# Splitting x times g_mix before its norm is known, and multiplying the norm's root in later, in the opening of a two-block transformer kernel

## The chip, the cores and the metric

The kernel runs on one core of one Trainium2 chip, in one launch. The metric is device time in microseconds (us), the median of several runs. The engines are TensorE (PE, matmuls; PEld its weight loads), VectorE (DVE), ScalarE (ACT), GpSimd (POOL) and SyncE (SP, which only issues transfers here).

## The reference, cut to what matters

Two transformer blocks over 1024 tokens of width 1024, in fp32. The first one begins so:

```python
def rms_norm(x, g):
    xf = x.astype(jnp.float32)
    y = xf * lax.rsqrt(jnp.mean(xf * xf, axis=-1, keepdims=True) + EPS)
    return (y * g.astype(jnp.float32)).astype(x.dtype)
...
        u = rms_norm(h, g_mix[l]) @ w_in[l]
        # u is cut into qa, ka, va (differential attention: 4 units of 128 columns each)
        # and qs, ksb, vs (stick-breaking attention: 4 units of 128 columns each)
        qa = apply_partial_rope(qa, cos, sin)
        ka = apply_partial_rope(ka, cos, sin)
        ya = diff_attention(qa, ka, va, lam, g_subln[l], lam_init)
        yb = stick_breaking_attention(qs, ksb, vs)
```

The root of the norm is one number per token. It is the same for all columns of a projection, and the rotation (apply_partial_rope) is linear, so it may be multiplied in before the projection or behind it.

## The kernel before, in words

**Layout.** Activations lie feature-major: 128 partitions hold features, the free dimension holds the 1024 tokens, in 8 slices k of 128 features and two halves h of 512 tokens. x is `hT`. Every product is made of three fp32r matmuls per slice (`product`, lines 184 to 186): the operand is split into a rounded high part and a low part (the rest), and high by high, high by low and low by high are summed. A chunk is one projection of 128 columns for 512 tokens, so 8 slices of three matmuls. It is named (what, unit, half): ("q",0,1) is q of unit 0, second half. "r" is a product with the rotation's matrix (parts 0 and 1 for q, 2 and 3 for k), "t" the transposition of v, "ada" and "o" are small ones. Chunks alternate between two PSUM banks; chunk n waits until chunk n-2 was taken out. Chunks run in the order of `CHUNK_ORDER`, which begins with `FIRST_CHUNKS`: q00, k00, q01, r00, r01, k01, r02, r03, v00, v01, t00, t01 (what, unit, part).

**Weights.** SP brings a panel of 512 KB into `w_raw`, GpSimd makes its high part (L233) and its low part (L194), into one of two places. A place is free again when the first matmul of the next panel has run (`weight_free`). SP asks for a panel when the one before was split.

**Opening.** The transfers of x come in 16 pieces. ScalarE squares each slice (L290) into `yT`; VectorE adds slices 4 to 7 of the first half (L328); TensorE sums over features with a matmul by ones (L337, L319 for the second half, put between the slices of q00); ScalarE takes Ln and Exp of the mean (`norm_root`, L345, L349). Only then VectorE multiplies x by g_mix and the root (L393), ScalarE takes the high part (L190), VectorE the low part (L194, in place of x), and TensorE starts the slice of q00. Then come k00, q01 and so on. VectorE also makes the angles (L2921 to L2936), ScalarE their sine and cosine (L3165, L3166), and VectorE rotates q and k of unit 0 (`rope_dve`, L703 to L706, three instructions of 1024 columns each for q and for k). The first scores of the attention (`da_scores(0)`, L744) wait for both.

**Attention stages.** 32 steps of differential attention (4 units of 8 steps, `da_pe`, `da_dve`, `da_act`) and then 48 of stick-breaking (4 units of 12 steps, `sb_...`) work on unit i while TensorE fills its time with the chunks of unit i+1. In every step TensorE issues scores, the chunks, a transposition of weights (L756, L911) and the product with v (L767, L929), in an order written out by hand; so do the other engines. In these stages all chunks are taken from PSUM by ScalarE (`chunk_act`, L678 for q and k, L674 for v, L670 for t), at the end of its step. VectorE's step: maxima, a third of a panel of the adaptive projection (`ada_dve`, four instructions from L691 to L697), rotation in steps 5 and 6, weights (L822, L824, L829); in stick-breaking two scans (L1013), a subtraction (L1019), `ada_dve` in some steps.

Of the kernel before, what the change touches and what calls it, by code (L numbers as in the profile page):

```python
# [99 lines left out]
def program(nc, xT_d, memT_d, pos_d, vec_d, const_d, bias_d, lora_d, w_d, out_d):  # L100
# [7 lines left out]
    with ctx:  # L108
# [166 lines left out]
        MIX_SUM = 3  # L275
        NORM_ADDS = {n: [(k, 0) for k in range(MIX_SUM + 1, KC)] if n == "mix" else [(k, h) for k, h in NORM_SQUARES[n] if k % KC and not summed_late(n, k, h)] for n in NORM_SQUARES}
        NORM_ROOTS = {"mix": [0, 1], "mem": [0], "x": [0, 1], "mlp": [0, 1], "fin": [0, 1], "fin1": [0, 1], "post": [0, 1]}
        NORM_OUT = {n: [(k, h) for h in (NORM_ROOTS[n]) for k in range(KC)] for n in NORM_SQUARES}
# [36 lines left out]
        def norm_pe_chunk(pe, n, h, k):  # L315

            c = norm_cols(n, h)
            pe.wait_ge(S("norm_sq_ready"), norm_at(NORM_SQUARES, n, (k, h)))
            m = pe.matmul(PS[:, NB + c.start:NB + c.stop], cst("ones"), norm_sq[n](k)[:, c], start=(k == 0), stop=(k == KC - 1))  # L319
            if k == KC - 1:  # L320
                m.then_inc(S("norm_summed"), 1)

        def mix_add(dve, k):
            dve.wait_ge(S("norm_sq_ready"), norm_at(NORM_SQUARES, "mix", (k, 0)))
            if k > MIX_SUM + 1:
                dve.wait_ge(S("norm_added"), norm_at(NORM_ADDS, "mix", (k - 1, 0)))
            c, sq = norm_cols("mix", 0), norm_sq["mix"]
            dve.tensor_tensor(sq(MIX_SUM)[:, c], sq(MIX_SUM)[:, c], sq(k)[:, c], ALU.add).then_inc(S("norm_added"), 1)  # L328

        def mix_sum_pe(pe):  # L330
            c = norm_cols("mix", 0)
            for k in range(MIX_SUM + 1):
                if k < MIX_SUM:
                    pe.wait_ge(S("norm_sq_ready"), norm_at(NORM_SQUARES, "mix", (k, 0)))
                else:
                    pe.wait_ge(S("norm_added"), norm_at(NORM_ADDS, "mix", (KC - 1, 0)))
                m = pe.matmul(PS[:, NB + c.start:NB + c.stop], cst("ones"), norm_sq["mix"](k)[:, c], start=(k == 0), stop=(k == MIX_SUM))  # L337
            m.then_inc(S("norm_summed"), 1)
# [154 lines left out]
        n_rs = arena[:, at_da:at_da + T]  # L493
# [107 lines left out]

        def chunk_done(c):

            return S("proj_evac"), CHUNK[c] + 1
# [16 lines left out]
        def chunk_pe(pe, c, part=None):  # L621
            n, (what, w, h) = CHUNK[c], c
            b = bank(n % 2)
            if n >= 2 and part != 1:
                pe.wait_ge(S("proj_evac"), n - 1)
# [19 lines left out]
            else:  # L645
# [4 lines left out]
                if w == 0 and what == "q":  # L650
                    def ready(k):
                        if h == 0:
                            norm_pe_chunk(pe, "mix", 1, k)
                        wait_split(pe, "mix", h)(k)
# [4 lines left out]
        def chunk_act(act, c):  # L659
            n, (what, w, h) = CHUNK[c], c  # L660
            if what == "w" or c == ("ada", UNITS - 1, 0):
                return
# [10 lines left out]
            elif what == "v":  # L673
                e = act.activation(raw[:, 4 + h, :], b, ACT.Copy)  # L674
            else:
                x = UNIT_PANEL[what]
                dst = (raw_qk if w < N_DA else heads(w))[x]
                e = act.activation(dst[:, cols], b, ACT.Copy, scale=0.125 if what == "q" else 1.0)  # L678
# [157 lines left out]
        def da_dve(dve, g):  # L836
# [11 lines left out]
            da_weights(dve, g)  # L848

# [6 lines left out]
        AT = [t.rearrange("p (h k) -> p h k", h=2) for t in (ar.take(T), pos_f)]  # L856
# [57 lines left out]
        def sb_values(pe, g):  # L914
# [12 lines left out]
            for b in range(n):  # L927
                for hd in range(2):
                    m = pe.matmul(PS[64 * hd:64 * hd + 64, 7 * HALF + t % 4 * P:7 * HALF + (t % 4 + 1) * P],  # L929
                                  values_of(w)[1][:, lo + b, 64 * hd:64 * hd + 64], AT[g % 2][:, hd, b * P:(b + 1) * P],  # L930
# [2575 lines left out]
```

## Time and profile before

| | us |
|---|---|
| median of 3 runs | 2319.09 (2318.38 to 2323.09) |
| the profiled execution: its time | 2321.39 |
| the profiled execution: its span | 2319.6 |
| TensorE busy | 2229.3 (96%) |
| VectorE busy | 1363.4 (59%) |
| ScalarE busy | 951.7 (41%) |
| GpSimd busy | 700.3 (30%) |
| first scores (L744) start at | 73.59 |

Times in the rows are microseconds from the start of the span. The opening is what lies ahead of the first scores. Differential attention runs up to about 330 us, stick-breaking up to about 620 us; the rest of the span is not touched by the change. "Busy" of TensorE includes matmuls at half clock and small ones, so 96% does not say that nothing can be gained.

### The profile page before, as it was taken

What the parts mean: (1) busy time and instruction counts of PE and PEld (TensorE: products, weight loads), DVE (VectorE), ACT (ScalarE), POOL (GpSimd) and SP (SyncE); (2) the same over time, 40 slices, a digit from 0 to 9 for tenths busy, and PEclk for the clock granted to TensorE, in tenths of its full rate; (3) what the DMA queues carried; (4) which work ended last, traced back from release to release, by engine and by line L of the source; (5) the groups of instructions that cost most, each with busy time, mean ns of one, the idle gap of its engine ahead of it and who ended that gap; (6) DMA issues with size and microseconds to landing.
All of it is one profiled execution on the core that took longest, in us unless ns stands there. A gap on an engine that the chain in (4) does not pass through costs nothing.

```text
span 2319.6 us, 36425 instructions
## 1 busy us (share of the span) xinstructions
PE 2229.3 (96%) x14780; PEld 1761.7 (76%) x14780; DVE 1363.4 (59%) x1775; ACT 951.7 (41%) x1688; POOL 700.3 (30%) x436
## 2 busy tenths in 40 slices
PE   7999999998999999999999999999899999999997
PEld 4777766666689887778888888888676787778885
DVE  6767647667677444575664575423508476567554
ACT  4443457677535223253344234233416412264321
POOL 2312211211221223345564564322141133222231
PEclk9999999999999999999999999999999999999999
DMA  3211101113023101111111111112120011100022
GB/s 132 73 55 55 37 28 55 55 46 119 26 93 119 37 28 37 46 37 55 64 36 54 54 54 45 55 46 96 64 79 28 19 37 37 39 19 13 4 110 82
DMA packets 38555, 125.80 MB, mean 54 GB/s; under 512 B 3856, under 2 KB 4368, under 8 KB 37776
## 3 DMA queue, kind: packets, MB, share of 16 engines
q1 hardware_dynamic: 33936, 103.30, 13.2%
q10 hardware_dynamic: 4480, 20.49, 2.3%
q8 instruction: 106, 1.74, 0.3%
q14 instruction: 33, 0.27, 0.0%
HBM read 114.34 MB, written 8.91 MB: 53 GB/s over the span
## 4 chain that ended last, share of the span: by engine, by line
PE 85%; DVE 8%; ACT 5%; issue 2%; DMA 0%; ACTq 0%; DVEq 0%
PE PS L184 22%; PE PS L186 22%; PE PS L185 22%; PE PS L2261 2%; PE PS L744 2%; PE PS L767 1%; PE PS L1200 1%; PE PS L929 1%; PE PS L894 1%; DVE arena L1013 1%; PE PS L911 1%; PE PS L312 1%; PE PS L1871 1%; DVE arena L393 1%; PE PS L1731 1%
## 5 line engine op out<-in xcount | busy, mean ns | idle before, releaser
L184 PE MATMUL PS<-u_r,w_hi 128*128 128x512 f32 x1184 | 480.5, 406 | 16.1 <-DVE h L581 3.6
L233 POOL TENSOR_TENSOR w_hi<-w_raw,const 128x1024 fp32r<-128x1024 f32 x77 | 152.0, 1974 | 1120.8 <-PE PS L184 1016.5
L186 PE MATMUL PS<-u_r,w_lo 128*128 128x512 f32 x1184 | 464.3, 392 | 0.0
L194 POOL TENSOR_TENSOR w_lo<-w_raw,w_hi 128x1024 fp32r<-128x1024 f32 (+1 forms) x143 | 331.3, 2317 | 325.4 <-ACT w_hi L190 310.5
L185 PE MATMUL PS<-arena_r,w_hi 128*128 128x512 f32 (+1 forms) x888 | 332.7, 375 | 0.0
L184 PEld LDWEIGHTS PS<-u_r,w_hi 128*128 128x128 f32 x1184 | 224.0, 189 | 72.8 <-DVE arena_r L194 6.5
L186 PEld LDWEIGHTS PS<-u_r,w_lo 128*128 128x128 f32 x1184 | 223.8, 189 | 48.1
L184 PE MATMUL PS<-h_r,w_hi 128*128 128x512 f32 x512 | 208.1, 406 | 4.7 <-DVE u_r L401 4.4
L185 PE MATMUL PS<-y_r,w_hi 128*128 128x512 f32 x512 | 201.3, 393 | 0.0
L186 PE MATMUL PS<-h_r,w_lo 128*128 128x512 f32 x512 | 199.6, 390 | 0.0
L1526 DVE TENSOR_TENSOR h<-h,PS 128x512 f32<-128x512 f32 x288 | 181.7, 682 | 21.8 <-PE PS L186 17.6
L185 PEld LDWEIGHTS PS<-arena_r,w_hi 128*128 128x128 f32 x888 | 167.8, 189 | 29.7 <-issue 0.7
L185 PE MATMUL PS<-h_r,w_hi 128*128 128x512 f32 x384 | 150.0, 391 | 0.0
L185 PE MATMUL PS<-u_r,w_hi 128*128 128x512 f32 x384 | 150.0, 391 | 0.0
L1013 DVE TENSOR_TENSOR_SCAN arena<-arena 128x512 f32<-128x512 f32 (+3 forms) x96 | 105.7, 1142 | 70.8 <-ACT arena L987 70.8
L1512 DVE TENSOR_TENSOR arena<-arena 128x512 f32<-128x512 f32 x60 | 51.4, 880 | 154.3 <-ACT arena L1445 154.3
L184 PE MATMUL PS<-y_r,w_hi 128*128 128x512 f32 x344 | 134.3, 390 | 0.0
L186 PE MATMUL PS<-y_r,w_lo 128*128 128x512 f32 x344 | 133.9, 389 | 0.0
L184 PEld LDWEIGHTS PS<-h_r,w_hi 128*128 128x128 f32 x512 | 96.1, 188 | 37.3 <-DVE u_r L401 8.1
L190 ACT ACTIVATE w_hi<-w_raw 128x1024 fp32r<-128x1024 f32 (+1 forms) x73 | 64.3, 881 | 132.4 <-PE PS L184 85.7
L185 PEld LDWEIGHTS PS<-y_r,w_hi 128*128 128x128 f32 x512 | 97.2, 190 | 20.4 <-issue 1.0
L186 PEld LDWEIGHTS PS<-h_r,w_lo 128*128 128x128 f32 x512 | 96.2, 188 | 20.7
(434 smaller groups left out, 4283.2 us busy)
## 6 DMA issues: line engine op xcount, KB each, us to landing
w_raw<-in_w SPq DMA_DIRECT2D x174, 512.0 KB, 3.4
arena<-in_w SPq DMA_DIRECT2D x10, 512.0 KB, 5.1
h<-in_xT ACTq DMA_DIRECT2D x1, 4096.0 KB, 14.6
u<-parked_stream ACTq DMA_DIRECT2D x1, 4096.0 KB, 12.9
out<-arena SPq DMA_DIRECT2D x16, 256.0 KB, 2.0
parked_stream<-h ACTq DMA_DIRECT2D x6, 512.0 KB, 2.6
h<-in_xT SPq DMA_DIRECT2D x8, 256.0 KB, 7.1
h<-in_xT ACTq DMA_DIRECT2D x8, 256.0 KB, 8.9
```

What stands on the lines that cost most here:

```text
L184: first = pe.matmul(out, a[0], b[0], start=start, stop=False)
L185: pe.matmul(out, a[0], b[1], start=False, stop=False)
L186: return first, pe.matmul(out, a[1], b[0], start=False, stop=stop)
L190: return e.activation(out, x, ACT.Copy)
L194: return e.tensor_tensor(out, x, hi_part.bitcast(F), ALU.subtract)
L233: pool.tensor_tensor(out, src, cst("ones")[:, 0:1].broadcast_to([P, D]), ALU.mult).then_inc(S("w_high"), 1)
L312: m = pe.matmul(PS[:, at + c.start:at + c.stop], cst("ones"), norm_sq[table](k)[:, c], start=(x == 0), stop=(x == len(parts) - 1))
L744: pe.matmul(bank(2 + 2 * c, 2)[:, lo:hi], q[r, s * P:(s + 1) * P], k[r, lo:hi], start=True, stop=(hi < kw))
L1013: m = dve.tensor_tensor_scan(sums, sums, ab[:, g % 2, hd, :cols][:, ::-1], 0.0 if whole else sp[:, (g - 1) % 2, hd, 0:1], ALU.add, ALU.add)
L1512: dve.tensor_tensor(*(st_block(f, x) for f in (out, a, b)), op).then_inc(S("hid_ready"), 1)
L1526: dve.tensor_tensor(dst, dst, bank((7 * j + p) % 8), ALU.add if sign > 0 else ALU.subtract).then_inc(S("dn_evac"), 1)
L2261: m = pe.matmul(out[half(cp), h, t, :], a(h, t)[half(cp), :], b(h, t)[half(cp), :], start=start, stop=stop)
```

## The change

1. **The split comes ahead of the root.** ScalarE makes the high part of x times g_mix directly from x (an activation with g_mix as its scale), and squares the slice right behind it. VectorE makes the low part in one instruction, x times g_mix minus the high part. The multiplication by the root (L393, 16 instructions) goes.
2. **The root is multiplied in later.** The sine and cosine tables are multiplied by it (two instructions of 1024 columns), which covers q and k of units 0 to 3. Every v, and q and k of units 4 to 7, are taken from PSUM by VectorE with a multiplication by the root (`scaled_chunk_dve`), where ScalarE copied them before: 16 v chunks and 16 of q and k. In `da_dve` this stands behind the weights of the step, in `sb_dve` behind the subtraction and `ada_dve`. For unit 0 the order on VectorE is: tables, rotation of q, v00, rotation of k, v01.
3. **Sums.** First half: TensorE sums slices 0 to 3 ahead of q00 and the rest (three additions on VectorE) ahead of q01. Second half: six additions on VectorE, two sums on TensorE ahead of k01, in place of eight sums between the slices of q00. The roots are taken by ScalarE behind the chunks q01 and r01.
4. **Order on ScalarE.** The second half's slices 0 to 3, then the chunk q00, then slices 4 to 7.
5. **Panel 1** (k of unit 0) is brought at the start, ahead of the late pieces of x, to a place of its own (`early_raw`), and split by GpSimd without a wait for TensorE; before, its split began with q00's first matmul.
6. The root lies in the place of the positions (`pos_f`) up to the end of stick-breaking, so its second weight buffer (`AT`) moves elsewhere.

```diff
         def split_unit_panel(pool, m):
-            if m > 0:
+            if m == 1:
+                pool.wait_ge(S("mem_in"), 16)
+                pool.sem_inc(w_in[0], 16)
+                pool.tensor_tensor(w_hi[:, 1, :], early_raw, cst("ones")[:, 0:1].broadcast_to([P, D]), ALU.mult).then_inc(S("w_high"), 1)
+                pool.wait_ge(S("w_high"), 2)
+                low(pool, w_lo[:, 1, :], early_raw, w_hi[:, 1, :]).then_inc(S("w_split"), 1)
+                return
+            if m > 1:
                 pool.wait_ge(S("weight_free"), m + CREDIT)
...
+        MIX_SUMS = {0: [(4, 5), (4, 6), (4, 7)], 1: [(0, 1), (2, 3), (4, 5), (6, 7), (0, 2), (4, 6)]}
...
+        def scaled(c):
+
+            return c[0] == "v" or (c[0] in "qk" and c[1] >= N_DA)
+
         def chunk_done(c):
 
-            return S("proj_evac"), CHUNK[c] + 1
+            same = [x for x in CHUNK_ORDER if scaled(x) == scaled(c)]
+            return S("proj_scaled" if scaled(c) else "proj_evac"), same.index(c) + 1
+
+        def scaled_chunk_dve(dve, c):
+
+            n, (what, w, h) = CHUNK[c], c
+            cols = slice(h * HALF, (h + 1) * HALF)
+            dve.wait_ge(S("proj_mm"), n + 1)
+            if what == "v":
+                e = dve.tensor_tensor(raw[:, 4 + h, :], bank(n % 2), n_rs[:, cols], ALU.mult)
+            elif what == "q":
+                e = dve.scalar_tensor_tensor(heads(w)[0][:, cols], bank(n % 2), 0.125, n_rs[:, cols], ALU.mult, ALU.mult)
+            else:
+                e = dve.tensor_tensor(heads(w)[1][:, cols], bank(n % 2), n_rs[:, cols], ALU.mult)
+            e.then_inc(S("proj_scaled"), 1)
...
             if n >= 2 and part != 1:
-                pe.wait_ge(S("proj_evac"), n - 1)
+                pe.wait_ge(*chunk_done(CHUNK_ORDER[n - 2]))
...
             da_weights(dve, g)
+            for c in da_chunks(i, s):
+                if scaled(c):
+                    scaled_chunk_dve(dve, c)
...
             load_main(0)
+            sync.dma_start(early_raw, w_d[2, :, :]).then_inc(S("mem_in"), 16)
             for k in range(4):
                 sync.dma_start(hT[:, k, HALF:T], xT_d[:, k, HALF:T]).then_inc(S("x_late"), 16)
-            load_main(1)
...
-            split_dve(dve, "mix", 0, in_(hT), in_u, in_h, mix)
+            for h in range(2):
+                for k in range(KC):
+                    mix_low(k, h)
+                for to, k in MIX_SUMS[h]:
+                    mix_add(dve, h, to, k)
...
-            dve.wait_ge(S("ang_ready"), 3)
+            dve.wait_ge(*norm_ready("mix", 1))
+            for x, table in enumerate((sinT, cosT)):
+                dve.wait_ge(S("ang_ready"), x + 2)
+                dve.tensor_tensor(table, table, n_rs, ALU.mult).then_inc(S("ang_step"), 1)
+            dve.wait_ge(S("ang_step"), 9)
             for x in range(2):
                 rope_dve(dve, 0, x)
-            dve.wait_ge(S("cact_ready"), 1)
+                scaled_chunk_dve(dve, ("v", 0, x))
+            dve.wait_ge(S("cact_ready"), 2)
...
+            def mix_part(k, h):
+                lo, hi = split_cols("mix", h)
+                act.activation(in_u(k, lo, hi), hT[:, k, lo:hi], ACT.Identity, scale=vcol("g_mix", k)).then_inc(S("split_high"), 1)
+                norm_square(act, "mix", k, h, hT[:, k, lo:hi])
...
             for k in range(KC):
-                mix_square(k, 1)
-                mix_split(0, [k])
-            norm_root(act, "mix", 1, n_rs)
-            for c in FIRST_CHUNKS:
+                mix_part(k, 1)
+                if k == 3:
+                    chunk_act(act, ("q", 0, 0))
+            act.wait_ge(S("const_in"), 16)
+            for c in FIRST_CHUNKS[1:]:
                 chunk_act(act, c)
-                if c == ("q", 0, 0):
-                    mix_split(1, range(KC))
+                if c in (("q", 0, 1), ("r", 0, 1)):
+                    mix_root(0 if c[0] == "q" else 1)
...
-            mix_sum_pe(pe)
-            pe.wait_ge(S("lam_exp"), 1)
+            mix_sum_pe(pe, 0, range(4), True, False)
             for c in FIRST_CHUNKS:
+                if c == ("q", 0, 1):
+                    mix_sum_pe(pe, 0, [4], False, True)
+                if c == ("k", 0, 1):
+                    mix_sum_pe(pe, 1, [0, 4], True, True)
```

## Rows read from the trace of the kernel before

**Rows 1.** The page: the chain that ended last, share by engine.
```profile
PE 85%; DVE 8%; ACT 5%; issue 2%; DMA 0%; ACTq 0%; DVEq 0%
```

**Rows 2.** Stretches: busy of each engine (x instructions), PEclk, DMA share, GB/s.
```profile
16.00:18.00 2.00, 0.37 (x1) 0.37 (x2) 1.38 (x2) 0.00 (x0) 0.00 (x0) 0.50 0.98 413
...
24.00:26.00 2.00, 2.00 (x6) 1.20 (x4) 2.00 (x3) 1.27 (x3) 1.62 (x1) 0.50 0.00 0
...
40.00:50.00 10.00, 9.41 (x40) 6.88 (x39) 9.87 (x17) 5.55 (x9) 0.00 (x0) 1.00 0.01 2
```

**Rows 3.** Timeline of the opening: start, duration, engine, line, [idle before <-releaser].
```profile
8.17 2.19 ACT L290 ACTIVATE y<-h 128x512 f32<-128x512 f32 x4
8.85 4.59 PE L337 MATMUL PS<-y,const 128*128 128x512 f32 x6 [3.23 <-ACT y L290]
...
12.29 2.35 POOL L194 TENSOR_TENSOR w_lo<-w_raw,w_hi 128x1024 fp32r<-128x1024 f32 x1
12.30 5.27 DVE L328 TENSOR_TENSOR y<-y 128x512 f32<-128x512 f32 x4 [7.58 <-ACT y L290]
...
38.36 0.40 PE L184 MATMUL PS<-u_r,w_hi 128*128 128x512 f32 x1
```

**Rows 4.** Instructions on the tile h: min/median/max ns, first and last start.
```profile
L393 DVE SCALAR_TENSOR_TENSOR h<-h,vec,arena x16: 736/742/2383, 21.3 to 47.6; 128x512 f32<-128x512 f32 x16
```

**Rows 5.** Timeline from k01's first matmul to the first scores.
```profile
52.33 0.56 PE L184 MATMUL PS<-u_r,w_hi 128*128 128x512 f32 x1
...
55.98 2.39 POOL L194 TENSOR_TENSOR w_lo<-w_raw,w_hi 128x1024 fp32r<-128x1024 f32 x1
...
62.16 1.89 POOL L233 TENSOR_TENSOR w_hi<-w_raw,const 128x1024 fp32r<-128x1024 f32 x1 [3.80 <-DMA w_raw<-in_w]
...
62.93 1.14 ACT L3166 ACTIVATE arena<-arena,const 128x1024 f32<-128x1024 f32 x1
...
64.16 3.46 DVE L703 TENSOR_TENSOR arena<-arena 128x1024 f32<-128x1024 f32 x1 [8.05 <-ACT arena L3166]
...
69.92 1.22 DVE L703 TENSOR_TENSOR arena<-arena 128x1024 f32<-128x1024 f32 x1
...
73.59 0.49 PE L744 MATMUL PS<-arena 64*128 64x128 f32 x4 [1.25 <-DVE arena L706]
```

**Rows 6.** Line 1526, a VectorE instruction with one operand in PSUM: min/median/max ns.
```profile
L1526 DVE TENSOR_TENSOR h<-h,PS x240: 678/680/690, 1033.5 to 1393.1; 128x512 f32<-128x512 f32 x120
```

**Rows 7.** Timeline of steps 5 and 6 of unit 0, differential attention.
```profile
111.78 3.25 POOL L194 TENSOR_TENSOR w_lo<-w_raw,w_hi 128x1024 fp32r<-128x1024 f32 x1
112.82 3.30 DVE L706 TENSOR_TENSOR y<-y,arena 128x1024 f32<-128x1024 f32 x1
...
116.94 1.02 DVE L829 SCALAR_TENSOR_TENSOR arena<-arena,er 128x768 f32<-128x768 f32 x1
...
118.65 0.60 PE L756 MATMUL PS<-const,arena 128*128 128x128 f32 x4
```

**Rows 8.** Timeline of the border between two units of stick-breaking.
```profile
401.52 0.61 ACT L674 ACTIVATE arena<-PS 128x512 f32<-128x512 f32 x1
...
403.81 1.05 PE L715 MATMUL PS<-const,arena 128*128 128x128 f32 x8
...
404.17 1.22 DVE L1019 TENSOR_TENSOR arena<-PS,arena 128x1024 f32<-128x1024 f32 x1
...
406.08 0.50 PE L184 MATMUL PS<-u_r,w_hi 128*128 128x512 f32 x1 [1.23 <-ACT arena L670]
```

**Rows 9.** Timeline of the border ahead of the last unit of stick-breaking.
```profile
544.23 1.05 PE L715 MATMUL PS<-const,arena 128*128 128x128 f32 x8
...
546.24 1.22 DVE L1019 TENSOR_TENSOR arena<-PS,arena 128x1024 f32<-128x1024 f32 x1
...
547.52 0.70 PE L894 MATMUL PS<-arena 64*128 64x256 f32 x4 [0.62 <-DVE arena L1019]
...
567.92 0.50 PE L184 MATMUL PS<-u_r,w_hi 128*128 128x512 f32 x1 [2.93 <-DVE h L581]
```

More of the change, by code:

```diff
@@ L272, in summed_late @@
             return n in ("mlp", "fin", "post") and h == 1 and k % KC >= KC - 2
-        MIX_SUM = 3
-        NORM_ADDS = {n: [(k, 0) for k in range(MIX_SUM + 1, KC)] if n == "mix" else [(k, h) for k, h in NORM_SQUARES[n] if k % KC and not summed_late(n, k, h)] for n in NORM_SQUARES}
+        MIX_SUMS = {0: [(4, 5), (4, 6), (4, 7)], 1: [(0, 1), (2, 3), (4, 5), (6, 7), (0, 2), (4, 6)]}
+        NORM_ADDS = {n: [(k, h) for h in range(2) for _, k in MIX_SUMS[h]] if n == "mix" else [(k, h) for k, h in NORM_SQUARES[n] if k % KC and not summed_late(n, k, h)] for n in NORM_SQUARES}
         NORM_ROOTS = {"mix": [0, 1], "mem": [0], "x": [0, 1], "mlp": [0, 1], "fin": [0, 1], "fin1": [0, 1], "post": [0, 1]}
-        NORM_OUT = {n: [(k, h) for h in (NORM_ROOTS[n]) for k in range(KC)] for n in NORM_SQUARES}
+        NORM_OUT = {n: [(k, h) for h in (NORM_ROOTS[n]) for k in range(KC)] if n != "mix" else [] for n in NORM_SQUARES}
         norm_sq = {}
@@ L330, in mix_sum_pe, with mix_add @@
[L330 to L338, printed above, removed]
+        def mix_add(dve, h, to, k):
+            c, sq = norm_cols("mix", h), norm_sq["mix"]
+            dve.wait_ge(S("norm_sq_ready"), norm_at(NORM_SQUARES, "mix", (k, h)))
+            before = [x for x in MIX_SUMS[h][:MIX_SUMS[h].index((to, k))] if x[0] in (to, k)]
+            if before:
+                dve.wait_ge(S("norm_added"), norm_at(NORM_ADDS, "mix", (before[-1][1], h)))
+            dve.tensor_tensor(sq(to)[:, c], sq(to)[:, c], sq(k)[:, c], ALU.add).then_inc(S("norm_added"), 1)
@@ new lines, in mix_sum_pe @@
+        def mix_sum_pe(pe, h, parts, start, stop):
+            c = norm_cols("mix", h)
+            for k in parts:
+                if stop and k == parts[0]:
+                    pe.wait_ge(S("norm_added"), norm_at(NORM_ADDS, "mix", (MIX_SUMS[h][-1][1], h)))
+                elif not stop:
+                    pe.wait_ge(S("norm_sq_ready"), norm_at(NORM_SQUARES, "mix", (k, h)))
+                m = pe.matmul(PS[:, NB + c.start:NB + c.stop], cst("ones"), norm_sq["mix"](k)[:, c], start=start and k == parts[0], stop=stop and k == parts[-1])
+            if stop:
+                m.then_inc(S("norm_summed"), 1)
@@ L672, in chunk_act @@
                 e = act.activation(osq[:, cols], b, ACT.Ln, bias=cst("eps"), scale=1.0 / P)
-            elif what == "v":
-                e = act.activation(raw[:, 4 + h, :], b, ACT.Copy)
             else:
                 x = UNIT_PANEL[what]
-                dst = (raw_qk if w < N_DA else heads(w))[x]
-                e = act.activation(dst[:, cols], b, ACT.Copy, scale=0.125 if what == "q" else 1.0)
+                e = act.activation(raw_qk[x][:, cols], b, ACT.Copy, scale=0.125 if what == "q" else 1.0)
             e.then_inc(S("proj_evac"), 1)
@@ L855, in program, with sb_at @@
         Eb = ar.take(2 * T).rearrange("p (b h k) -> p b h k", b=2, h=2)
-        AT = [t.rearrange("p (h k) -> p h k", h=2) for t in (ar.take(T), pos_f)]
+        at_even = ar.take(T)
+        def sb_at(g):
+            t = at_even if g % 2 == 0 else yT[:, 7, :] if g < 3 * SB_N else arena[:, 14 * T + 3 * P:15 * T + 3 * P]
+            return t.rearrange("p (h k) -> p h k", h=2)
         def sb_item(g):
@@ L1030, in sb_dve @@
                     ada_dve(dve, *at[j, s])
-                if j == 3:
-                    for c in sb_chunks(j, s):
-                        if c[0] != "t":
-                            late_chunk_dve(dve, c)
+                for c in sb_chunks(j, s):
+                    if scaled(c):
+                        scaled_chunk_dve(dve, c)
+                    elif j == 3 and c[0] != "t":
+                        late_chunk_dve(dve, c)
             else:
```

57 lines of the change are left out of this document (22 added, 35 removed).

## Prediction

> **What bounds the kernel now.** I read the chain that ended last first. It runs over TensorE for 85% [rows 1], so the change pays only where TensorE starts earlier or waits less. Then I read the granted clock by stretches, the timeline of the opening engine by engine, and the waits of TensorE in the two attention stages.
>
> In the opening the reader sees a chain that is not TensorE's: x lands, ScalarE squares, VectorE adds, and here it stands still behind GpSimd. Its four additions take 5.27 us [rows 3], of which the first waits for the low part of panel 0, which began 0.01 us before it and took 2.35. Then come the sum, the root, and three passes per slice on two engines. k00's first matmul is at 38.36 [rows 3], k01's at 52.33, the first scores at 73.59 [rows 5]. From there TensorE hardly waits.
>
> The trace shows one thing that matters for everything below: a VectorE instruction with two operands in SBUF and a GpSimd instruction exclude each other, and they take turns. In rows 7 GpSimd's low part (3.25 in place of 2.35) waited for the VectorE instruction ahead, and VectorE's next (3.30 in place of 1.22) waited for GpSimd. The low part beside the cosine did the same to L703: 3.46 against 1.22 [rows 5]. With an operand in PSUM this is not so: 240 instructions of L1526 took 0.678 to 0.690 [rows 6].
>
> **Part 1, up to k01.** ScalarE now makes two passes per slice. Four squares took 2.19, so 0.53 each [rows 3], 1.07 per slice; slices 0 to 7 are squared by 9.3, 10.4, ... 16.8. TensorE's sums of slices 0 to 3 take 2 passes each of 0.77 to 0.86 (six passes took 4.59 [rows 3]), so from 9.4 to 16.2, which is before it can do much else.
>
> The low parts are one instruction each of 0.74 (the form of L393 [rows 4]), the first at 9.4. From 10.3 GpSimd splits panel 0, and now panel 1 directly behind it: 1.89 + 2.35 + 1.89 + 2.39 = 8.5 us [rows 3, 5] of GpSimd work. Both engines are never idle together and take turns, so the last of seven remaining low parts ends at 10.3 + 8.5 + 7 x 0.64 = 23.3. Without this collision it would be 17.5. q00's last slice ends at 24.4 (at half clock at 26). So k00 starts at 24.4 where it started at 38.36.
>
> From k00's to k01's first matmul it took 13.97 us: 48 matmuls at 0.235 (40 in 9.41 [rows 2]) are 11.3, four passes for the rotations 1.7, and about 1 us is waiting for low parts. Now the wait is gone (the low parts of the second half end at about 31, when q01 starts), and six passes of sums at 0.43 are added, 2.6 us. That is 15.6, and k01 starts at 40.0: 12.3 us earlier. Hidden under TensorE here: the additions on VectorE (9 x 0.7), ScalarE's roots (2 x 1.4), panel 1's split. Panel 1's transfer delays the late pieces of x by 0.5 MB, about 2.5 us by the rate of this stretch; ScalarE then needs them at 17 and has until 24. If that cover went, ScalarE would be late by that much at most.
>
> **Part 2, from k01 to the first scores.** Before, the cosine ended 11.7 us after k01's start (52.33 to 64.07 [rows 5]). The same queue stands ahead of it, so it ends at 51.7 and the sine at 50.6. Then comes a longer chain on VectorE: two tables (2 x 1.2), rotation of q (3 x 1.2), v00 (0.68 [rows 6]), rotation of k (3 x 1.2), v01 (0.68), 11.0 us together, where it was 7.0. And again GpSimd meets it: the low part of panel 2 ends at about 46.5, the raw panel 3 lands 3.8 us later (58.37 to 62.16 [rows 5]), so both halves of panel 3's split fall on the two table instructions. Two blocks, 4.0 us; bounds: 0 and 4.3. v01 is out at 65.5, TensorE turns t01 in 0.6, the first scores start at 66.1. Gain 7.5 (between 6 and 11.5).
>
> What is late next: TensorE. It has done v01's matmuls at 58.2 and then waits 2.5 us for v00 and 4 us for v01, for t00 and t01 need them. In the trace an idle stretch of such length, from 13.4 (the end of the six passes) to 17.6 (the end of the additions) [rows 3], goes with a granted clock of 0.50, at 1.2 GHz, from 16 until 26, four us after TensorE was busy again [rows 2]. I charge the same: four us at half clock on matmuls that bound the step, 2 us (bounds 0 and 2.5). The Trainium skill ("TensorE: Matmul & The Clock Gate", Part 1) calls the throttled state the default, which only activity releases; by that rule the new wait costs this second charge, without it the opening would be worth the whole first gain. The trace agrees with it at 16 to 26 us. Opening: -7.5 + 2 = -5.5 (between -11.5 and -2.5).
>
> VectorE's step 0 starts about 1 us later against the scores than before, as ScalarE loads two tables behind t01. TensorE's next need of it is more than 1 us away; nothing.
>
> **Part 3, the chunks taken by VectorE.** The instruction costs 0.68 instead of 0.60 and isn't blocked [rows 6]; what matters is its place in the queue. In differential attention it follows the weights. In step 5 these end at 117.96, so v0 is out at 118.6, and TensorE asks for that bank after L756 of 118.65, at 119.1 [rows 7]: no wait, by 0.5 us. The other steps have more room. Nothing.
>
> In stick-breaking it follows the subtraction of its step. At a border between units ScalarE took v1 at 401.52, and TensorE turned v at 403.81 [rows 8]. Now v1 waits for the subtraction, which ends at 405.4, and is out at 406.1; t0 follows, ScalarE takes it, and q's first matmul is at 407.3 instead of 406.08. 1.2 us, twice. At the third border VectorE is busy without a pause: v0's 0.68 shifts the subtraction of 546.24 to 546.9, v1 is out at 548.8, t1 ends at 549.4 instead of 545.3, and the scores of 547.52 come 1.7 us behind it, at 551.1 [rows 9]. ScalarE stands behind them. The stretch up to the wait of 2.93 at 567.92 is bound by ScalarE and VectorE, so 3.3 us go through to the end. In three steps VectorE's extra 0.68 is on a chain that ScalarE's saved 0.5 nearly pays back: 0.2 x 3 = 0.6. Sum +6.3, less 0.3 for what ScalarE saves elsewhere: +6.0 (between +2.5 and +8).
>
> **The sum.** -7.5 + 2 + 6.0 = +0.5 on the profiled execution's 2321.39, so 2321.9. That execution lies 2.3 above the median of the runs, 2319.09; against the median I say 2319.5. About 0.2%, 4.6 us, is what a measurement of this kernel can tell from no change.
>
> **The rivals.** *The opening keeps its gain (faster).* GpSimd's split of panel 3 misses the tables, for instance because panel 2 was split earlier: 4 us more. Then TensorE's waits are 1 to 3 us and the clock may hold, 2 us more; the sum is -5.5, 2313.6. For it: the blocks come from a coincidence of about 1 us. Against: GpSimd's start hangs on TensorE and SP in the same way as the sine does, so the meeting place is steady. 0.27.
>
> *v of differential attention comes too late (slower).* In step 5 the margin is 0.5 us. If VectorE is later by more, TensorE waits ahead of v1 in each of three units, and by one more turn with GpSimd (2 us and more, as in rows 7) this is 3 x 2 = 6 us: 2325.5. It decides from 0.5 us of lateness. Against: GpSimd has already blocked VectorE twice in this very step. 0.16.
>
> *The high parts don't wait for a root, but nothing comes earlier.* If TensorE stayed at half clock through q00 and k00, k01 would start 1.6 + 5.6 = 7.2 us later than I say (24 matmuls at twice 0.235), and the opening be worth nothing: +7.7, 2326.8. Against: the sums from 9.4 on keep TensorE busy. It shares the chance above; its milder form, q00 alone, is in my forecast's range (2321.1).
>
> Forecast (little change, between 2315 and 2323.5): 0.57. Faster by over 0.2% 0.27, within 0.2% 0.57, slower 0.16. The range for 8 in 10 takes most of the faster case and half of the slower: 2311 to 2324.
>
> **What would show it.** In the profile after: low parts of 0.74 with four or so of 2.5 to 3 us between 10 and 23 us; k00's first matmul near 24.4, k01's near 40; two table multiplications of 3 us near 51 to 57; L744 first near 66 with idle time of TensorE ahead of it and a granted clock of 0.5 behind; TensorE waiting ahead of the transposition of v at the borders of units, and the third border 3 us longer. If the first scores start under 63, or the borders show no wait, the number is too high; if TensorE waits ahead of the second half of v in differential attention, it is too low.

## The result, and the profile after

The changed kernel takes 2328.6 us (median of 9 runs, 2324.53 to 2332.52), the kernel before 2320.94 in the runs beside it (9 runs, 2318.38 to 2323.09). The ratio is 1.0034, with a 95% interval from 1.0026 to 1.0043: slower by 7.7 us. I had said 2319.5, and a range that ends at 2324. Of the 9.1 us between, 1.9 lie in the kernel before, whose median I took from 3 runs (2319.09) and which is 2320.94 with 9; the other 7.2 are the change's. The profiled execution of the changed kernel took 2328.1.

The shares on the profile's page have hardly moved, and show nothing of it [rows 1]:

```profile
PE 2228.9 (96%) x14770; PEld 1762.3 (76%) x14770; DVE 1385.0 (60%) x1798; ACT 936.3 (40%) x1656; POOL 703.0 (30%) x436
...
PE 85%; DVE 8%; ACT 5%; issue 2%; DMA 0%; SPq 0%; DVEq 0%; ACTq 0%
```

VectorE has 21.6 us more work and ScalarE 15.4 less, TensorE as much as before.

The opening does what was said, within about 1 us at each mark. These are rows of its timeline after the change (start, duration, engine, line, and in brackets the idle time before):

```profile
11.04 11.78 DVE L2943 SCALAR_TENSOR_TENSOR h_r<-h,vec,u_r 128x512 fp32r<-128x512 f32 x7 [0.38 <-ACT y L297]
...
12.51 2.68 POOL L194 TENSOR_TENSOR w_lo<-w_raw,w_hi 128x1024 fp32r<-128x1024 f32 x1
...
17.58 2.70 POOL L194 TENSOR_TENSOR w_lo<-arena,w_hi 128x1024 fp32r<-128x1024 f32 x1
...
24.53 0.49 PE L184 MATMUL PS<-u_r,w_hi 128*128 128x512 f32 x1
...
40.28 0.79 PE L184 MATMUL PS<-u_r,w_hi 128*128 128x512 f32 x1
...
50.30 1.89 POOL L233 TENSOR_TENSOR w_hi<-w_raw,const 128x1024 fp32r<-128x1024 f32 x1 [3.92 <-DMA w_raw<-in_w]
...
51.74 4.87 DVE L2977 TENSOR_TENSOR arena<-arena,pos_i 128x1024 f32<-128x1024 f32 x2 [5.15 <-ACT arena L3205]
...
60.17 0.68 DVE L621 TENSOR_TENSOR arena<-PS,pos_i 128x512 f32<-128x512 f32 x1
...
61.00 0.63 PE L731 MATMUL PS<-const,arena 128*128 128x128 f32 x4 [1.93 <-DVE arena L621]
...
65.13 1.09 PE L731 MATMUL PS<-const,arena 128*128 128x128 f32 x4 [3.49 <-DVE arena L621]
66.15 0.80 PE L760 MATMUL PS<-arena 64*128 64x128 f32 x4
```

The seven low parts share the time with GpSimd, q00 ends and k00 starts at 24.5 (38.36 before [rows 3]), k01 starts at 40.28 (52.33 [rows 5]), GpSimd meets the two tables, TensorE waits 1.93 and 3.49 for v, and the first scores start at 66.15 (73.59 [rows 5]). What is lost is lost in stick-breaking. Here are rows of its timeline. L731 turns v, L184 begins a chunk, L918 are scores, L1043 is VectorE's subtraction, L621 and L625 are its copies of v and k with the root multiplied in. They answer to [rows 8, 9]:

```profile
399.64 0.68 DVE L621 TENSOR_TENSOR arena<-PS,pos_i 128x512 f32<-128x512 f32 x1
...
400.38 1.97 PE L731 MATMUL PS<-const,arena 128*128 128x128 f32 x8 [2.08 <-DVE arena L621]
...
402.18 0.79 PE L184 MATMUL PS<-u_r,w_hi 128*128 128x512 f32 x1
...
472.77 1.10 PE L731 MATMUL PS<-const,arena 128*128 128x128 f32 x8 [2.08 <-DVE arena L621]
...
520.04 1.22 DVE L1043 TENSOR_TENSOR arena<-PS,arena 128x1024 f32<-128x1024 f32 x1
...
521.18 0.68 DVE L625 TENSOR_TENSOR arena<-PS,pos_i 128x512 f32<-128x512 f32 x1
...
521.91 0.50 PE L184 MATMUL PS<-u_r,w_hi 128*128 128x512 f32 x1 [2.41 <-DVE arena L625]
...
523.68 0.63 PE L184 MATMUL PS<-u_r,w_hi 128*128 128x512 f32 x1
524.10 0.63 PE L185 MATMUL PS<-h_r,w_hi 128*128 128x512 f32 x1
...
548.48 1.22 DVE L1043 TENSOR_TENSOR arena<-PS,arena 128x1024 f32<-128x1024 f32 x1
...
549.62 0.68 DVE L621 TENSOR_TENSOR arena<-PS,pos_i 128x512 f32<-128x512 f32 x1
...
550.45 1.09 PE L731 MATMUL PS<-const,arena 128*128 128x128 f32 x4 [3.82 <-DVE arena L621]
...
554.14 0.70 PE L918 MATMUL PS<-arena 64*128 64x256 f32 x4
```

Four times TensorE stands still for a copy of VectorE's, for 2.08, 2.08, 2.41 and 3.82 us. Stretches of the same execution (busy of PE, PEld, DVE, ACT, POOL, then the granted clock, DMA share and GB/s) show what follows such a wait:

```profile
22.00:24.00 2.00, 2.00 (x6) 1.61 (x5) 1.90 (x4) 0.76 (x2) 0.00 (x0) 0.50 0.52 197
...
66.00:68.00 2.00, 2.00 (x10) 1.47 (x9) 0.00 (x0) 1.73 (x2) 0.11 (x1) 0.50 0.00 0
68.00:70.00 2.00, 2.00 (x8) 1.60 (x7) 1.59 (x3) 1.96 (x5) 1.92 (x2) 0.72 0.00 0
...
398.00:404.00 6.00, 3.92 (x16) 3.11 (x15) 2.94 (x5) 2.67 (x6) 0.95 (x1) 0.72 0.01 3
472.00:478.00 6.00, 4.99 (x36) 3.89 (x36) 1.36 (x4) 1.35 (x3) 3.22 (x2) 1.00 0.00 0
518.00:524.00 6.00, 3.59 (x21) 2.92 (x20) 5.80 (x6) 3.59 (x7) 1.51 (x1) 0.92 0.00 0
524.00:530.00 6.00, 6.00 (x35) 3.85 (x35) 2.44 (x2) 1.39 (x2) 3.56 (x2) 0.79 0.01 3
...
548.00:554.00 6.00, 3.56 (x24) 2.90 (x24) 2.91 (x5) 1.77 (x4) 0.00 (x0) 0.72 0.91 391
```

After three of the four waits the granted clock falls; after the second it doesn't (1.00). In the kernel before it was 1.00 in the stretches of the first and of the last wait:

```profile
398.00:404.00 6.00, 5.86 (x46) 4.81 (x45) 3.77 (x4) 5.17 (x9) 0.00 (x0) 1.00 0.00 0
...
548.00:554.00 6.00, 4.39 (x41) 2.68 (x40) 4.09 (x6) 6.00 (x10) 0.00 (x0) 1.00 1.02 436
```

A way to read both kernels side by side is to take the start of each step's scores in the changed kernel and subtract that of the kernel before (73.59 at the first step, 547.52 at step 37 of stick-breaking, and so on; steps are counted through the four units, from 0). The difference stays the same over many steps and then jumps; a jump upwards is a loss with a place, one downwards a gain. Below, "first" and "next" are the first two steps of differential attention, "SB 0" and "SB 47" the first and last of stick-breaking, and the four columns between are the jumps from step 12 to 13, 24 to 25, 32 to 33 and 36 to 37 (the first, second and fourth stand at the borders between units). All from one execution each, in us:

| kernel | first | next | SB 0 | 12-13 | 24-25 | 32-33 | 36-37 | SB 47 | median |
|---|---|---|---|---|---|---|---|---|---|
| changed | -7.44 | -6.10 | -6.56 | +2.42 | +1.27 | +3.79 | +4.83 | +6.33 | 2328.6 |
| changed, again (e8) | -7.98 | -6.51 | -6.97 | +2.42 | +3.70 | +4.82 | +4.87 | +9.43 | 2329.77 |
| e1, copies alone | +0.19 | +0.21 | -0.21 | +2.33 | +3.66 | +4.80 | +5.15 | +16.13 | 2335.18 |
| e2, opening alone | -9.09 | -8.05 | -9.39 | -0.01 | -0.01 | +0.02 | -0.09 | -9.82 | 2312.99 |
| e3, copies first | -7.74 | -6.35 | -6.78 | -0.01 | -0.02 | -0.31 | +0.51 | -7.65 | 2311.89 |
| e4, panel 3 later | -11.18 | -6.32 | -5.75 | +2.50 | +2.26 | +3.85 | +5.09 | +9.85 | 2332.28 |
| e5, borders first | -8.71 | -7.40 | -7.87 | +0.02 | -0.02 | +3.80 | +1.05 | -2.33 | 2317.5 |
| e6, k first, once | -8.41 | -7.23 | -8.05 | +3.73 | +2.54 | -0.31 | +5.15 | +0.87 | 2325.77 |
| e7, e3 and v first | -7.85 | -5.75 | -6.50 | +0.00 | -0.01 | -0.30 | +0.50 | -6.93 | 2313.9 |

The jumps left out of the table that are over 0.8 us lie at fixed steps too. They don't hang on the place of the copies in stick-breaking, for e3 has them as well: from first to next, then -1.4, +1.6 and -1.6 at the borders between the units of differential attention, and +1.6 from step 2 to 3 of stick-breaking (e6 lacks this one and has -1.65 from step 0 to 1; some kernels lack others). The clock goes with them, in either kernel. At the -1.4 and the -1.6 it is the kernel before that runs slower, 0.73 from 132 to 138 us and 0.75 from 262 to 268, where the changed kernel has 1.00. At the +1.6 between them it is the changed kernel, 0.72 from 190 to 196, where the kernel before has 1.00. At the last one it is 0.76 from 339 to 345 us in the changed kernel and 0.74 in e8, and 1.00 in the kernel before. Twice one of 1.1 to 1.5 stands behind step 40 (+1.07 in e4, -1.54 in e2).

Behind stick-breaking the two kernels run the same program, and the difference still wanders, by 0.4 to 3.5 us: +6.33 becomes +6.7 at the end of the span for the changed kernel (2326.3 less 2319.6), -9.82 becomes -12.0 in e2 (2307.6 less 2319.6), -2.33 becomes +0.7 in e5 (2320.3). So medians say what a version is worth, and jumps say where.

### The profile page after: what moved, and what is told of

It is laid out like the page before. It is cut to its first block, busy times and chain, and to the rows that moved or that the text cites. A ratio compares the mean times of both kernels' runs of the same rounds, so it can differ in the third digit from the quotient of the medians.

```text
span 2326.3 us, 36417 instructions
## 1 busy us (share of the span) xinstructions
PE 2228.9 (96%) x14770; PEld 1762.3 (76%) x14770; DVE 1385.0 (60%) x1798; ACT 936.3 (40%) x1656; POOL 703.0 (30%) x436
## 4 chain that ended last, share of the span: by engine, by line
PE 85%; DVE 8%; ACT 5%; issue 2%; DMA 0%; SPq 0%; DVEq 0%; ACTq 0%
PE PS L184 22%; PE PS L186 22%; PE PS L185 22%; PE PS L2286 2%; PE PS L760 1%; DVE arena L1037 1%; PE PS L783 1%; PE PS L1225 1%; PE PS L918 1%; PE PS L953 1%; PE PS L319 1%; PE PS L935 1%; DVE arena L396 1%; PE PS L1896 1%; PE PS L1756 1%
## 5 line engine op out<-in xcount | busy, mean ns | idle before, releaser
L184 PE MATMUL PS<-u_r,w_hi 128*128 128x512 f32 x1184 | 479.5, 405 | 17.1 <-DVE h L585 4.4
L184 PEld LDWEIGHTS PS<-u_r,w_hi 128*128 128x128 f32 x1184 | 224.6, 190 | 70.5 <-DVE arena_r L194 6.6
L184 PE MATMUL PS<-h_r,w_hi 128*128 128x512 f32 x512 | 209.9, 410 | 4.3 <-DVE u_r L404 4.0
L184 PE MATMUL PS<-y_r,w_hi 128*128 128x512 f32 x344 | 134.2, 390 | 0.0
L184 PEld LDWEIGHTS PS<-h_r,w_hi 128*128 128x128 f32 x512 | 96.9, 189 | 37.6 <-issue 8.4
## 6 DMA issues: line engine op xcount, KB each, us to landing
u<-parked_stream ACTq DMA_DIRECT2D x1, 4096.0 KB, 12.9
```

The source lines that it names most:

```text
L184: first = pe.matmul(out, a[0], b[0], start=start, stop=False)
```

## The experiments

The first four ran together on one chip, the other four on another, each beside the kernel before (2320.97 and 2320.94).

**1. Only the copies** (e1): the opening of the kernel before, and VectorE takes v of units 1 to 7 and q and k of units 4 to 7 at the places where the changed kernel takes them. The root is in x already, so it multiplies by one.

```diff
+            one = cst("ones")[:, 0:1].broadcast_to([P, HALF])
...
+                e = dve.tensor_tensor(raw[:, 4 + h, :], bank(n % 2), one, ALU.mult)
...
-                pe.wait_ge(S("proj_evac"), n - 1)
+                pe.wait_ge(*chunk_done(CHUNK_ORDER[n - 2]))
```

> The kernel before, with its opening untouched, in which VectorE instead of ScalarE takes the v chunks of units 1 to 7 and the q and k chunks of units 4 to 7 from PSUM, in the same instructions and places as the change has them, but multiplied by one. Theory 1 (the place in VectorE's queue): no gain in the opening, and the losses that the trace after shows in stick-breaking, between the scores of steps 12 and 13 (+2.4), 24 and 25 (+1.3), 32 and 33 (+3.8), 36 and 37 (+4.8), so +10 to +13 against before. Rival A (the granted clock's luck in the rest of the kernel makes the difference): no more than +3. Rival B (the losses come from what else moved: the root in pos_f, the second weight buffer, the early panel): within 2 of before.

Measured: 2335.18, ratio 1.0051 (1.0038 to 1.0064), +14.2 us. The four jumps stand where they stand in the changed kernel; the only other one over 1 us in its stick-breaking is the +1.6 from step 2 to 3, which e2 and e3 have too. What VectorE's copies cost is 14 us, not the 6 of my sum.

**2. Only the opening** (e2): the changed kernel, but ScalarE copies every chunk except v of unit 0. This version leaves the root out of v of units 1 to 7 and of q and k of units 4 to 7, so its time says what the opening is worth, and it is no kernel to use.

```diff
         def scaled(c):
-            return c[0] == "v" or (c[0] in "qk" and c[1] >= N_DA)
+            return c[0] == "v" and c[1] == 0
...
+            elif what == "v":
+                e = act.activation(raw[:, 4 + h, :], b, ACT.Copy)
```

> The change, but ScalarE copies all v, q and k chunks behind unit 0's v as it did before, so that the root is left out of v of units 1 to 7 and of q and k of units 4 to 7; the new opening, the scaled tables and v of unit 0 stay. Theory 1: the first scores at 66 as in the change, no new waits in stick-breaking, so -5 to -8 against before, 2313 to 2316. Rival A: between -2 and +8, as after. Rival B: slower than before as the change is, +3 to +8.

Measured: 2312.99, ratio 0.9969 (0.9956 to 0.9981), -8.0 us, and none of the four jumps. With experiment 1 it is additive within the intervals: -8.0 + 14.2 = +6.2, beside +7.7 measured for both.

**3. The copies ahead of the scans** (e3): the changed kernel, and in every step of stick-breaking VectorE takes the chunk first, then scans and subtracts. The same instructions, another order.

```diff
                 t, lo, n, cols = sb_item(g)
+                for c in sb_chunks(j, s):
+                    if scaled(c):
+                        scaled_chunk_dve(dve, c)
                 dve.wait_ge(S("sb_ln"), g + 1)
...
                 for c in sb_chunks(j, s):
-                    if scaled(c):
-                        scaled_chunk_dve(dve, c)
-                    elif j == 3 and c[0] != "t":
+                    if j == 3 and c[0] != "t" and not scaled(c):
```

> The change, with one thing moved: in stick-breaking VectorE takes the chunk of a step from PSUM ahead of the step's scans, not behind its subtraction and adaptive part. TensorE has finished the chunk by then, about 1 us before ScalarE's last instruction for the scans, so it fills idle time of VectorE. Theory 1: the waits of TensorE at the three borders of units and ahead of step 33 go, and -10 to -13 against the change, which is -3 to -7 against before. Rival A and B: no change against after. A third outcome, half of that: VectorE's extra 0.68 per chunk costs also where it is placed well.

Measured: 2311.89, ratio 0.9958 (0.9945 to 0.9971), -9.1 us against before, 16.7 under the changed kernel in its own runs. That is more than I expected (10 to 13). The first border in its timeline:

```profile
397.30 1.05 PE L731 MATMUL PS<-const,arena 128*128 128x128 f32 x8
...
399.58 0.50 PE L184 MATMUL PS<-u_r,w_hi 128*128 128x512 f32 x1 [1.23 <-ACT arena L689]
```

TensorE turns v without a wait, and in front of q it waits 1.23, as before the change [rows 8]. This version is the fastest complete kernel that I have.

**4. GpSimd's split of panel 3 held back** (e4), to keep it off the two multiplications of the tables.

```diff
                 pool.wait_ge(S("weight_free"), m + CREDIT)
+            if m == 3:
+                pool.wait_ge(S("qk_ready"), 2)
             split_panel(pool, m, 0, m, m % 2)
```

> The change, with GpSimd's split of panel 3 held until both rotations of unit 0 are done, so that it can't meet the multiplication of the two tables. If the turns with GpSimd cost VectorE 4 us there, the two table instructions take 1.2 each instead of 2.4 on average, the first scores start at 62 instead of 66, and q of unit 1 waits for its panel until about 66, which is 1 us earlier than now (67.0): -1 to -2 in all. If they don't matter, the first scores stay at 66, q of unit 1 begins at 70, and it is +3.

Measured: 2332.28, ratio 1.0048 (1.0035 to 1.0061), +11.3 against before, so 3 to 4 slower than the changed kernel. Its timeline:

```profile
50.51 2.36 DVE L2979 TENSOR_TENSOR arena<-arena,pos_i 128x1024 f32<-128x1024 f32 x2 [4.97 <-ACT arena L3207]
...
62.41 0.80 PE L762 MATMUL PS<-arena 64*128 64x128 f32 x4
...
65.24 0.77 PE L184 MATMUL PS<-u_r,w_hi 128*128 128x512 f32 x1 [1.70 <-POOL w_lo L194]
```

and its granted clock behind the scores:

```profile
66.00:68.00 2.00, 2.00 (x7) 1.52 (x6) 1.86 (x6) 0.76 (x4) 0.00 (x0) 0.50 0.81 258
68.00:70.00 2.00, 2.00 (x6) 1.59 (x5) 0.62 (x2) 0.00 (x0) 1.38 (x1) 0.50 0.57 178
```

The two multiplications take 2.36 in place of 4.87, and the first scores start at 62.41. So the meeting with GpSimd is real, and it costs 2.5 us. The other 1.2 of the 3.7 by which the scores are earlier than in the changed kernel are no work of this edit: here, as in e2, e5 and e6, q00 and k00 ran at full clock, and the tables begin at 50.51 in place of 51.74. One such row, of e2, to be read against the row of 22.00 above:

```profile
22.00:24.00 2.00, 2.00 (x10) 1.62 (x9) 1.90 (x4) 0.56 (x2) 0.00 (x0) 1.00 0.42 160
```

But the next chunk, q of unit 1, now waits for the panel that was held back (1.70), and it starts at half clock. A step later the offset is -6.32, where it was -6.10: the 3.7 us are gone. Against the executions whose opening ran at the same clock (-8.05, -7.40 and -7.23) it is 0.9 to 1.7 us behind. As made, the edit shows only that the split has no room behind the scores either; a release just behind the tables wasn't tried. The rest of what the median has lost isn't explained.

**5 to 8.** These ran together: the copy first only in the last step of each unit (e5), only in step 7 of the third unit (e6), experiment 3 with v ahead of the rotations in the opening (e7), and the changed kernel once more (e8). The edits, around the loop of experiment 3:

```diff
+                early = s == SB_N - 1          # e5
+                early = (j, s) == (2, 7)       # e6
+                for c in sb_chunks(j, s):
+                    if scaled(c) and early:
+                        scaled_chunk_dve(dve, c)
                 dve.wait_ge(S("sb_ln"), g + 1)
...
                     if scaled(c):
-                        scaled_chunk_dve(dve, c)
+                        if not early:
+                            scaled_chunk_dve(dve, c)
...
             for x in range(2):                 # e7
-                rope_dve(dve, 0, x)
                 scaled_chunk_dve(dve, ("v", 0, x))
+                rope_dve(dve, 0, x)
```

> The changed kernel, and only in the last step of each stick-breaking unit VectorE takes the chunk ahead of the step's scans; everywhere else it stays behind the subtraction. Theory (place in VectorE's queue, step by step): the gaps that opened at the three borders (+2.4, +1.3 and +4.8 us between the scores ahead and behind) vanish, and the gap of +3.8 in front of step 33 stays, with TensorE's wait of 2.4 us there. That is 6 to 8.5 us faster than the changed kernel, so 2320 to 2323. Rival (one queue position is as good as another, and what the third experiment gained came from all steps together, through less work of VectorE behind the subtraction): the borders keep half of their losses or more, 2324 to 2327.

Measured: 2317.5, ratio 0.9979 (0.997 to 0.9989), 12.3 under e8. (One of its 11 runs took 12353.86 us, and nothing here explains it; without it the median is 2317.2.) The jumps at the first two borders are gone, that at the third falls to +1.05, and +3.80 at step 33 stays. I had expected 6 to 8.5, from the jumps of one trace; by those of e8 it is 2.4 + 3.7 + 3.8 = 9.9, and at SB 47 the two traces are 11.8 apart, 0.9 of it from the opening (SB 0).

> The changed kernel, and only in step 7 of the third stick-breaking unit VectorE takes the chunk (the second half of k) ahead of the scans. Theory: only the gap of +3.8 in front of step 33 vanishes, with the wait of 2.4 us for that bank; the three borders keep +2.4, +1.3 and +4.8. That is 3 to 4 us faster than the changed kernel, 2324 to 2326. Rival (that wait is only a symptom of lateness which reaches that step from the two borders before it): the gap shrinks by less than 1 us.

Measured: 2325.77, ratio 1.0021 (1.0012 to 1.003), 4.0 under e8. The jump at step 33 is gone (-0.31) and the three borders keep theirs. So that wait is no echo of the borders ahead of it: one instruction in one place of the queue, 4 us. Together e5 and e6 move four of the 18 copies and gain 12.3 + 4.0 = 16.3 us, nearly all of the 16.7 of experiment 3.

> The third experiment's kernel, and in the opening VectorE takes each half of v of unit 0 ahead of the rotation (v00, rotation of q, v01, rotation of k). Theory 1 of the opening (the order costs only what stands behind the last rotation): TensorE turns both halves of v while VectorE rotates k, so the first scores start 0.7 to 1.1 us earlier, near 65.2, and the wait of 3.5 us shrinks to about 1.5. If the half clock behind the first scores comes from the waits, the first step also loses less (0.5 in place of 1.3): together 1 to 1.8 us faster than the third experiment, 2310 to 2311. Rival (as with the fourth experiment, the clock takes back what is gained): the scores of step 1 stand where they stood, within 0.5 us, 2311 to 2313.

Measured: 2313.9, ratio 0.9966 (0.9952 to 0.9979), 2 us above experiment 3 where I expected a gain of 1 to 1.8. This comparison crosses two chips and the intervals overlap, so the size is not settled, but there is no gain to be seen. Its scores start at 65.74 (in e3 at 65.85), right behind the rotation of k, though its two tables were done 1.0 later (57.31 against 56.30). They began 0.56 later, behind an opening with a clock of 0.64 and 0.51 at 22 to 24 and 24 to 26 (0.50 and 0.88 in e3), and took 0.45 longer. So up to the scores the order may be worth the 0.7 to 1.1 that I had expected; this pair of traces can't tell. The clock stays low longer than behind the changed kernel's first scores:

```profile
68.00:70.00 2.00, 2.00 (x6) 1.56 (x5) 1.97 (x2) 0.01 (x1) 2.00 (x1) 0.50 0.00 0
70.00:72.00 2.00, 2.00 (x9) 1.61 (x9) 1.97 (x2) 0.00 (x0) 1.92 (x2) 0.92 0.04 8
```

Waits of 2.3 and 2.8 us (v, then the rotation of k) in place of 1.7 and 3.5 bring the same half clock, and the offset at the next step is -5.75 beside -6.35. So the rival of this experiment comes nearer than the theory, but it isn't met either: it wanted the next step within 0.5 (0.6) and 2311 to 2313.

> The changed kernel itself once more, timed beside the other three on the same chip, so that they can be compared within one call. Expected 2327 to 2330; with the same seven offsets from the kernel before in its trace: -7.4 at the first scores, -6.1 from step 1, four gaps in stick-breaking (+2.4, +1.3, +3.8, +4.8), each within 1 us. If the gaps move to other steps or are of other size by more than that, they are luck of one execution and not places of the queue.

Measured: 2329.77, ratio 1.0032 (1.0022 to 1.0041). The jumps are at the same four steps. Two are larger than in the first trace by more than the 1 us that I allowed, that at step 25 by 2.4 and that at step 33 by 1.0. The place is not luck, but the clock is: behind the wait of step 33 it is 0.53 from 524 to 530, 0.79 in the first trace. The second border in its timeline, to be read against the row of 472.77 above:

```profile
472.34 1.97 PE L731 MATMUL PS<-const,arena 128*128 128x128 f32 x8 [2.08 <-DVE arena L621]
474.14 0.80 PE L184 MATMUL PS<-u_r,w_hi 128*128 128x512 f32 x1
```

and its clock:

```profile
474.00:480.00 6.00, 6.00 (x30) 4.50 (x28) 0.00 (x0) 0.69 (x2) 4.27 (x2) 0.63 0.00 0
```

The same eight matmuls behind the same wait of 2.08 us take 1.97 here and 1.10 there, and the chunk behind them runs at 0.63. The jump is +3.70 here and +1.27 there. So 1.27 is what the wait costs against the kernel before, and the other 2.4 goes with the clock.

## Why the prediction was wrong, by its steps

**Up to k01: right.** The seven low parts end at 22.82 (11.04 + 11.78; I said 23.3), q00 at 24.5 (I said 24.4), and k01 starts 0.3 behind my 40.0. Taking turns with GpSimd is what makes them last that long: 1.68 each where 0.74 is the plain duration [rows 4]. The hits are in part luck. My sum put 0.64 for an instruction of 0.74, without a reason; with 0.74 it would have said 24.0. And it was made for full clock: this execution had 0.50 at 22 to 24, and in e2, with 1.00 there, k00 starts at 23.64.

**From k01 to the first scores: the mechanism right, the time partly luck.** Both halves of panel 3's split fell on the two tables, 4.87 us; experiment 4 undid it, and they took 2.36. So the meeting costs 2.5, where I had put 4.0. That the first scores still start at 66.15 (66.1) comes from two other misses: the tables begin at 51.74 (50.6), and t01 takes 1.09 at half clock (0.6). The gain is 7.44 (7.5). The half clock behind the scores took back 1.34 (-7.44 to -6.10), where I charged 2.

That a copy from PSUM with its other operand in SBUF is not blocked can't be read from L621: its 16 instructions took 0.676 to 0.690 us, but none of them ran beside a GpSimd instruction. L1526 of the kernel before [rows 6] shows it, nine at 0.68 each beside GpSimd's low parts:

```profile
1051.66 6.13 DVE L1526 TENSOR_TENSOR h<-h,PS 128x512 f32<-128x512 f32 x9 [0.67 <-PE PS L186]
...
1052.46 1.30 POOL L194 TENSOR_TENSOR w_lo<-w_raw,w_hi 128x512 fp32r<-128x512 f32 x1 [1.32 <-ACT w_hi L190]
1053.72 1.29 POOL L194 TENSOR_TENSOR w_lo<-comb,w_hi 128x512 fp32r<-128x512 f32 x1
```

The Trainium skill ("SBUF — State Buffer", Who interferes with whom) says that a VectorE instruction with two SBUF inputs contends with a GpSimd one that reads SBUF, and that one with at most one SBUF input, outside the modes that use both ports, does not. Both sides are seen here, 2.5 us on the two tables and nothing on L1526.

Seven executions with this opening and this order on VectorE put the first scores between 7.44 and 11.18 earlier. Without e4, which has no meeting with GpSimd, they fall in two groups by the clock of q00 and k00: 7.44, 7.74 and 7.98 with 0.50 at 22 to 24, and 8.41, 8.71 and 9.09 with 1.00 (e6, e5, e2). Experiment 2 makes the opening worth 8.0 by medians. I had -5.5. Of the 2.5 between, 0.7 is the charge for the clock; the rest is of the size of that scatter.

**Differential attention: right but for 0.7 us.** I had said that the copies cost nothing there, and named 0.5 us of margin in step 5 as the rival's place. The only wait for one of VectorE's copies in this stage is 0.44 us, and it is for k of unit 4; the offset grows by 0.7 at that step (27 to 28) in every kernel with these copies, and not in e2. The waits of TensorE there (releaser, total, times, longest) after the change:

```profile
PE PS L772 <- ACT arena L802: 5.5, 4, 1.4
...
PE PS L184 <- DVE arena L625: 0.4, 1, 0.4
```

The first is the same 5.5 as before. The slower rival did not happen; the time came out above its 2325.5 for another reason, so that it came out slower is no point for it.

**Stick-breaking: wrong, +6.0 in place of +12.9 (one trace, SB 0 to SB 47), +16.4 (the other), +14.2 (medians of e1).** The failed step is the third part's last paragraph: it left out one wait of TensorE for VectorE's copy (2.4 us), and it put the clock behind all of its waits at nothing (4.2 us in the first trace by subtraction, 5.6 to 7.8 in those of e4, e8 and e1).

*A wait that it doesn't have.* I went through the borders, for there the next unit's v is wanted at once, and gave the other steps 0.2 us each. But a chunk also waits until the chunk two before it has left its bank. In the third unit the small "ada" chunk runs in step 8 ahead of v's first half:

```python
            if s == (8 if j == 2 else 11 if j < 2 else None):
                parts += [(("ada", u, 0), None)]
...
            return parts + dense if s == 8 else dense + parts if s == 11 else parts + dense
```

So v's first half takes the bank of k's second half, which VectorE is to empty at the end of step 7, behind the subtraction (520.04, then 521.18). TensorE comes for it 2.41 us too early. In the first two units the "ada" chunk is in step 11, v's first half takes the bank of k's first half, long empty, and no wait is seen. The wait is 2.4 us in both traces. The jumps there are 3.8 and 4.8, for the clock falls behind it too: in the first trace the last seven matmuls of this part of the chunk start 0.43 apart (523.68, 524.10) and not 0.23, and 7 x 0.2 = 1.4 is the rest of the 3.8. Experiment 6 removes this wait alone, and its jump with it.

*The clock behind the waits.* The waits at the borders were sized nearly right: v of the first border is out at 400.32, with the offset of -5.67 there 405.99 on the old time, and I had said 406.1; at the third it is out at 550.30, with +1.79 that is 548.5 (548.8). At the second border of the first trace the clock held, and the jump is +1.27, where I said 1.2. At the first and second borders of the other kernels that keep these copies, and at the first of this trace, it is +2.26 to +3.73, and at the third +4.83 to +5.15 in place of 3.3. (The 3.3 has no working: my own rows give 551.1 less 547.52, which is 3.6.) I had charged the clock behind the waits of the opening and not behind these, though they are of the same length. Of the 12.3 us of jumps in the first trace, 1.2 + 1.2 + 3.3 = 5.7 are in my sum, 2.4 are the wait that I missed, and 4.2 are left for the clock, 2.8 at the three borders (1.2, 0.1 and 1.5) and 1.4 behind the missed wait. At the third border it can be counted: from the turning of v to the scores the same matmuls take 1.09, 1.98 and 0.85 us where they take 0.63, 1.09 and 0.66 at full clock. The Trainium skill ("TensorE: Matmul & The Clock Gate", Part 1) calls the throttled clock the default, which activity releases; the trace agrees in so far as the clock is low behind the waits, 0.72 at 398 to 404 and again at 548 to 554, where the kernel before had 1.00. But whether it falls behind such a wait can't be foretold from these runs: the same wait of 2.08 led to 1.00 once and to 0.63 once, and why is open.

*The sum.* With -8.0 and +14.2 it would have been +6.2 on the median, beside +7.7 and +8.8 measured in the two sets of runs. The rest of 1.5 to 2.6 is less than the 2.9 by which each of the two intervals reaches to a side; nothing here tells more of it. So the 7.2 by which the change missed its forecast are 8.2 too little for stick-breaking and this rest of 1.5, less 2.5 that the opening gained beyond my sum.

**The rivals.** The gain of the opening is kept, and a little more than in my forecast; that its loss to GpSimd could be had back was tried in one way (e4) and brought nothing. Half clock through q00 and k00 came only in its mild form, 0.50 at 22 to 24 and 1.00 from 26 on, and in e2, e4, e5 and e6 not at all. Experiment 3 lies at 2311.9, below my faster rival (2313.6), and for another reason than that rival's: what stood between the change and that time was the position of four copies in VectorE's queue.

## What to carry to other kernels

Before handing the emptying of PSUM to another engine, follow each bank and not only each value: list for every chunk who writes that bank next and when, for the wait that I missed is one of order in TensorE's queue and has nothing to do with who uses the data. On the new engine put the copy ahead of the long work of the step: the same instructions in another order were worth 16.7 us here, twice what the new opening gains. And count a new wait on TensorE with what the clock may add behind it: here 0 to 2.5 us for each wait of 2.1 to 4.3 us.

## What was unexpected of the hardware

- The same wait with the same instructions around it costs 1.27 or 3.70 us, by whether the granted clock falls behind it. So a single trace can miss what medians show, to either side: e2's execution lies 12.0 us under that of the kernel before and its median 8.0, the changed kernel's 6.7 over it and its median 7.7.
- Starting TensorE earlier can be worth nothing: in experiment 4 the first scores came 3.7 us earlier and the next step's only 0.2, with one more wait of 1.70 and at half clock (0.50 from 62 to 70 us).
- VectorE and GpSimd hold each other up where both have work queued and all operands lie in SBUF: seven low parts of 0.74 took 11.78 us beside four GpSimd instructions of 1.9 to 2.7. It doubles VectorE's tables (4.87 against 2.36 for two) and doesn't show where one operand of the VectorE instruction lies in PSUM (L1526, 0.678 to 0.690).
- The copies as such are nearly free in stick-breaking: all 18 ahead of the scans (e3) change the difference to the kernel before by only 0.9 us from SB 0 to SB 47 (-6.78 to -7.65).
